# A two-block transformer kernel: the opening, both mixing branches and their gates written as one stage

## The reference, cut to what matters

```
mod = silu(c) @ w_ada + b_ada;  sh1, sc1, g1, sh2, sc2, g2 = split(mod, 6)
h = rmsnorm(x, norm_mix) * (1 + sc1) + sh1
rq, rk, rv, rg, dq, dk, dv, gate_r, gate_d = split(h @ w_in)
ro = retention(rope(rq), rope(rk), rv)              # 4 heads, 128 / 256 wide
ret_out = (head_rms(ro) * silu(rg)) @ w_ret_o
do = softmax(q1 k1) v - lam * softmax(q2 k2) v      # causal, 4 heads
diff_out = (head_rms(do) * diff_norm * 0.8) @ w_diff_o
merged = sigmoid(gate_r) * ret_out + sigmoid(gate_d) * diff_out
x = x + g1 * (merged @ w_out)
```

## Time and profile before

| | us |
|---|---|
| median of 3 runs | 3007.53 |
| profiled execution | 3010.33 |
| its span | 3008.6 |
| TensorE busy in the span | 2784.9 |
| VectorE busy | 2032.0 |
| first product matmul of the first block starts at | 74.58 |
| last product matmul of the changed part ends at | 767.9 |

### The profile page before, as it was taken

One profiled execution on the slowest core, in us unless ns is written; L12 is line 12 of the kernel. 1 busy time (PEld: TensorE's weight loads), 2 busy tenths in 40 slices (PEclk: granted clock), 3 DMA queues, 4 the chain that ended last, 5 costly groups with the idle time before them and its releaser, 6 DMA issues. The chain is left out here.

```text
span 3008.6 us, 36105 instructions
## 1 busy us (share of the span) xinstructions
PE 2784.9 (93%) x14003; PEld 2438.9 (81%) x14003; DVE 2032.0 (68%) x2760; ACT 1376.3 (46%) x1853; POOL 955.8 (32%) x499
## 2 busy tenths in 40 slices
PE   5979898679799999998898899989999999999999
PEld 4747786357578888886386689989999999999999
DVE  4436572522378988985166369998888768888884
ACT  2213212322267787775134233448788733333332
POOL 0414443024112222231122135633333344444430
PEclk7989999789699999999988999999999999999999
DMA  5315522012289999997431224559999999999993
GB/s 208 109 49 202 197 84 84 0 42 70 101 308 365 380 390 371 357 359 300 189 121 36 70 71 126 178 169 327 352 350 341 348 375 359 377 374 374 369 366 109
DMA packets 171261, 703.98 MB, mean 234 GB/s; under 512 B 24624, under 2 KB 51920, under 8 KB 134736
## 3 DMA queue, kind: packets, MB, share of 16 engines
q1 hardware_dynamic: 87696, 460.01, 41.8%
q0 software_dynamic: 47232, 142.66, 12.8%
q10 hardware_dynamic: 36160, 98.97, 8.8%
HBM read 658.03 MB, written 72.88 MB: 243 GB/s over the span
## 5 line engine op out<-in xcount | busy, mean ns | idle before, releaser
L188 PE MATMUL psum<-h_high,pe_high 128*128 128x384 f32 (+1 forms) x1664 | 570.1, 343 | 11.5 <-DVE h_low L2404 9.2
L190 PE MATMUL psum<-h_high,pe_low 128*128 128x384 f32 (+1 forms) x1664 | 564.1, 339 | 0.0
L189 PE MATMUL psum<-h_low,pe_high 128*128 128x384 f32 (+1 forms) x1664 | 564.1, 339 | 0.0
L2140 ACT ACTIVATE pe_high<-ring 128x1024 fp32r<-128x1024 f32 x272 | 287.1, 1056 | 326.4 <-PE psum L190 326.2
L2267 DVE TENSOR_TENSOR pe_low<-ring,pe_high 128x1024 fp32r<-128x1024 f32 x216 | 264.5, 1225 | 199.1 <-ACT pe_high L2140 196.4
L167 POOL TENSOR_TENSOR slab_low<-half_slab,slab_high 128x1024 fp32r<-128x1024 f32 x88 | 219.3, 2496 | 502.2 <-ACT slab_high L158 472.2
L188 PEld LDWEIGHTS psum<-h_high,pe_high 128*128 128x128 f32 x1664 | 313.4, 188 | 17.3 <-issue 10.0
L1335 DVE TENSOR_TENSOR slab_low_moe<-half_slab_moe,slab_high_moe 128x2048 fp32r<-128x2048 f32 x126 | 285.7, 2288 | 52.1 <-ACT slab_high_moe L1284 52.1
L190 PEld LDWEIGHTS psum<-h_high,pe_low 128*128 128x128 f32 x1664 | 313.0, 188 | 5.2
L189 PEld LDWEIGHTS psum<-h_low,pe_high 128*128 128x128 f32 x1664 | 313.4, 188 | 4.6
L2025 POOL DMA_INDIRECT pe_rows<-in_v_rows,pe_place x128 | 203.9, 1593 | 257.8 <-DVE pe_sums L2374 222.5
(11 more groups left out here) (452 smaller groups left out, 5993.3 us busy)
## 6 DMA issues: line engine op xcount, KB each, us to landing
half_slab_moe<-in_weights SPq DMA_DIRECT2D x128, 1024.0 KB, 7.3
ring<-in_weights SPq DMA_DIRECT2D x162, 512.0 KB, 5.5
hT<-in_weights SPq DMA_DIRECT2D x64, 1024.0 KB, 7.3
ring<-in_v_rows SPq DMA_DIRECT2D x128, 512.0 KB, 7.2
half_slab<-in_weights SPq DMA_DIRECT2D x44, 1024.0 KB, 5.1
gates_rows<-pe_table ACTq DMA_DIRECT2D x12, 2048.0 KB, 10.5
pe_gt<-gates_rows ACTq DMA_DIRECT2D x16, 1536.0 KB, 23.3
gelu_rows<-pe_gl ACTq DMA_DIRECT2D x30, 768.0 KB, 5.9
```

What stands on the lines that cost most here:

```text
L188: pe.matmul(out, w[0], x[0], start=start, stop=False)
L189: pe.matmul(out, w[0], x[1], start=False, stop=False)
L190: return pe.matmul(out, w[1], x[0], start=False, stop=stop)
L2140: act.activation(high[:, g % RING, :], raw[:, g % RING, :], ACT.Copy).then_inc(highs, 1)
```

## The change

All seven blocks become one block, `stage_mixer`, with one semaphore for each hand-over and no barrier within.

- Opening. The shift part is no longer made on TensorE: w_shift and L352 go, and VectorE makes all 16 dot products (`dots(0)` to `dots(7)`, 1 MB of w_ada each, six buffers). The small loads change their order (the rope positions last, the table's inputs earlier), and the widening of the table's input goes from GpSimd to ScalarE. The squares go ahead of every other small ScalarE step but the silu. The rope angles and sines come after the split of h. The scaling and the remainder are interleaved by chunks (`scale_chunk(k + 1)`, `low_chunk(k)`), and the first product tile waits for each chunk by itself (`split`). GpSimd makes the first quarter of slab 0 early and the next three once six chunks of h are split.
- Retention. `scores(0)` go between the k slab and the v slabs, `scores(1)` behind the v slabs; in the loop, output(i), then scores(i + 2), then the sum of squares. The sum of the last head goes behind the first tile of the silu gate. The decay table loads behind slab 1.
- Gates and output of retention use banks 4 to 7, the next projection banks 0 to 3. The sigmoid goes straight into `merged` (a copy of 512 columns on VectorE for each of 8 tiles goes). The 32 dot products take 0.5 MB each from a ring of four, spread 1, 2, 1 a tile over 24 tiles instead of 2 over 16. c is not loaded and activated again.
- Attention. Units run in the order t = 0, 3, 1, 2. Scores(0) and (1) go ahead of the v slabs. In the loop, scores(u + 2) go before swap(u) (the transposes), needing only the exponents of unit u. Five of the eight gate tiles are computed between the units, in steps of one chunk (three matmuls), 3, 3 and 2 steps in turn. Their results are copied out by ScalarE, the sigmoids are taken in one row later. The split of a head's result into high and low comes within the loop for heads 0 to 2.
- The last two stages (output, joint output) keep their order of products.

```diff
+            r_scores_of(0)
+            tokens(S_RV, r_turned, 4)
+            tokens(S_RV + 1, r_valued, 0)
+            r_scores_of(1)
+            for i in range(HEADS):
+                r_output(i)
+                if i + 2 < HEADS:
+                    r_scores_of(i + 2)
+                if i + 1 < HEADS:
+                    r_total_of(i)
...
+            pe.wait_ge(merged_by, 8)
+            pe.wait_ge(d_turned, 10)
+            d_scores_of(0)
+            d_scores_of(1)
+            tokens(S_DV, d_turned, 12)
+            tokens(S_DV + 1, d_valued, 0)
+            steps = iter([(n, k) for n in range(FILLED) for k in range(DC)])
+            for u, (i, t) in enumerate(units):
+                if u + 2 < len(units):
+                    d_scores_of(u + 2)
+                if t == ORDER[0] and i >= 1:
+                    d_output(i - 1)
+                if t == ORDER[1] and i >= 1:
+                    d_total_of(i - 1)
+                for _ in range(STEPS[u]):
+                    n, k = next(steps)
+                    gate_steps(n, (k,))
+                swap(u)
+            d_output(HEADS - 1)
+            gate_steps(FILLED, range(0, 3))
+            d_total_of(HEADS - 1)
+            gate_steps(FILLED, range(3, DC))
+            for n in range(FILLED + 1, 8):
+                gate_steps(n, range(DC))
...
+            for t in range(6):
+                dots(t)
+            dve.wait_ge(root, 1)
+            chain(dve.reciprocal(rstd, rstd))
+            dots(6)
+            dots(7)
...
+            scale_chunk(0)
+            for k in range(DC):
+                if k + 1 < DC:
+                    scale_chunk(k + 1)
+                low_chunk(k)
...
+            for u, (i, t) in enumerate(units):
+                if u + 1 < len(units):
+                    softmax_max(u + 1)
+                mix(u)
+                if t == ORDER[2] and i >= 1:
+                    d_norm(i - 1)
+                if t == ORDER[3] and i >= 1:
+                    do_lows(i - 1)
```

More of the change, by code:

```diff
@@ L206, in pe_tokens @@
[L206 to L219, removed]
@@ new lines, in _ @@
+            pe.wait_ge(const_in, 16)
+            for k in range(DC):
+                pe.wait_ge(squares_sem, k + 1)
+                mm = pe.matmul(m.bank[4][:, :], m.ones, work[:, k, :], start=(k == 0), stop=(k == DC - 1))
+            mm.then_inc(total, 1)
+            pe.wait_ge(rel_widened, 1)
+            for i in range(SWA_HEADS):
+                if i >= 3:
+                    pe.wait_ge(dist_sb, i - 2)
+                pe.matmul(m.bank[5 + i % 3][:, 0:VEC], rel_wide[:, i, :], buckets, start=True, stop=True).then_inc(dist_mm, 1)
@@ L546, in _, with dots @@
             chain = lambda instruction: m.chain(dve, instruction)
+            def dots(t):
+                dve.wait_ge(ada_in[t % 6], 16 * (t // 6 + 1))
+                first = ada_columns(t)[0]
+                for i in range(2):
+                    chain(dve.tensor_tensor_reduce(
+                        out=junk, in0=ada[t % 6][:, i * D:(i + 1) * D], in1=c_act, scale=1.0,
+                        scalar=0.0, op0=ALU.mult, op1=ALU.add, accum_out=m.raw[:, first + i:first + i + 1]))
+                dve.sem_inc(dotted, 1)
@@ new lines, in r_norm, with mod_dots @@
+            def r_norm(i):
+                dve.wait_ge(r_root, i + 1)
+                chain(dve.reciprocal(r_std, r_std))
+                for c in range(2):
+                    last = dve.tensor_tensor(roT[:, 2 * i + c, :], r_bank[i % 2][c][:, :], r_std, ALU.mult)
+                last.then_inc(r_normed, 1)
+            def mod_dots(first, count):
+                for n in range(first, first + count):
+                    dve.wait_ge(ring_in[n % 4], 16 * (n // 4 + 1))
+                    chain(dve.tensor_tensor_reduce(
+                        out=junk, in0=ada_ring[n % 4], in1=c_act, scale=1.0, scalar=0.0, op0=ALU.mult, op1=ALU.add,
+                        accum_out=m.raw[:, 16 + n:17 + n]))
+                    dve.sem_inc(ada_used, 1)
+                return first + count
@@ L762, in total @@
-            def total(h):
-                pe.wait_ge(s.squares, 2 * (h + 1))
-                if h >= 1:
-                    pe.wait_ge(s.root, h)
-                for c in range(2):
-                    mm = pe.matmul(ss_bank[:, :], m.ones, squares[:, c, :], start=(c == 0), stop=(c == 1))
-                mm.then_inc(s.total, 1)
-            scores(0)
-            scores(1)
-            for u, (h, t) in enumerate(units):
-                if t == 0 and h >= 1:
-                    output(h - 1)
-                turn(u)
-                if u + 2 < len(units):
-                    scores(u + 2)
-                if t == 1 and h >= 1:
-                    total(h - 1)
@@ L869, in stage_route @@
+            for i in range(8):
+                m.wait_product(dve, S_OUT + i // 4, i % 4)
+                dve.scalar_tensor_tensor(out=m.xT[:, i, :], in0=m.bank[i % 4][:, :], scalar=m.mod[:, 16 + i:17 + i],
+                                         in1=m.xT[:, i, :], op0=ALU.mult, op1=ALU.add).then_inc(mix_done, 1)
 def stage_route(nc, m, xT, hT, scale, shift):
```

1131 lines of the change are left out of this document (521 added, 610 removed).

## The result

| | before | after |
|---|---|---|
| median, 4 runs each | 3007.82 (3006.81 to 3011.51) | 2896.52 (2893.23 to 2899.65) |
| ratio, 95% interval | 1 | 0.9628 (0.9611 to 0.9644) |
| profiled execution, its span | 3010.33, 3008.6 | 2899.65, 2897.6 |
| first product matmul starts | 74.6 | 43.9 |
| last joint output product ends | 767.9 | 654.4 |

The change takes 111.3 us away, where 119.8 were forecast. The profiled executions differ by 110.7 us, the changed part by 113.5. The untouched part behind it took 2240.7 us before and 2243.2 after; over the fourteen kernels profiled here it lay between 2236.4 and 2243.8, though its code is the same in all. So effects of a few us are read inside the changed part.

What follows compares the result with a forecast made beforehand. TensorE, busy 2784.9 of 3008.6 us, was taken as the bound, losing time to waits and low clock in opening, retention and attention. Savings 25.7 + 21.3 + 10.2 + 6.8 + 55.8 = 119.8 gave 2888 us, range 2874 to 2904 (8 in 10: 2862 to 2925).

Steps and rivals of the forecast that it cites:

- opening, first projection: Start to first projection's end, 167.0 us before: shift leaves TensorE, chunks start products earlier; 25.7 saved, bounds 15 to 30.
- retention: Retention, 59.3 us before: barriers out, scores moved ahead, 38.0 left with 3.5 of waits; 21.3 saved, bounds 14 to 24.
- gates, retention output: Gates and retention's output, 140.7 us before: VectorE's load, barrier and split wait go, six dense slabs 130.5; 10.2 saved.
- attention, gates, its output: Attention through its output, 215.0 us before: 24 us a head, loop 89.5, total 159.2; 55.8 saved, bounds 45 to 67.
- L352 goes: Opening: TensorE's 27.5 us of shift at half clock vanish; VectorE's eight more dots and a read cost some 10.4 us.
- by chunks: Opening: one scaling and one remainder per chunk of h; first chunk reaches TensorE at 41.9, the eighth put at 56.
- The collision with GpSimd: Opening's split: GpSimd's three quarters after chunk six meet VectorE; 2.07 us for one meeting, 2.1 added.
- the serial piece: Attention, each head: sum of squares, root, 4.9 us VectorE block, maximum, mix; about 10 us, 3 to 3.5 added.
- R1: Attention runs at TensorE's own pace, 67 saved there for 55.8; 135 saved in all, 2873 us; chance 0.14.
- R2: Attention: the chain in a unit stays the bound, 40 to 16 saved there instead of 55.8; 2915 us; chance 0.18.
- R3: Opening gives nothing: VectorE's dots or collisions move h back to 74.5, 25.7 less saved; 2913 us; chance 0.04.
- R4: Slower: interleaved stretches and slabs behind hold TensorE's clock at 0.50, some 20 us more a slab; 3048; chance 0.04.

Runs made afterwards that it cites:

- before_no_shift: Kernel before with 8 of its 64 one-column shift products on TensorE (features 128 to 1023 left out): ratio 0.9926 to the kernel before.
- first_tile_whole: Changed kernel where the first product tile waits for all eight chunks of h: ratio 0.9652 to the kernel before (changed kernel 0.9628).
- joint_by_chunks: Changed kernel; joint output's first tile waits chunk by chunk, ScalarE rounds the merged tile before the weights' next quarter: ratio 0.9607 to the kernel before (changed 0.9628).
- root_early: Changed kernel with ScalarE's root of a head's sum moved ahead of the copy of that unit's transposes: ratio 0.9601 to the kernel before (changed 0.9628).
- before_scores_first: Kernel before with attention's scores(u + 2) moved ahead of the output and transposes of unit u: ratio 0.9904 to the kernel before.

## Why the prediction was right, point by point

| stretch | saved, forecast | saved, measured |
|---|---|---|
| opening, first projection | 25.7 | 28.0 |
| retention | 21.3 | 23.8 |
| gates, retention output | 10.2 | 8.6 |
| second projection | 6.8 | 6.4 |
| attention, gates, its output | 55.8 | 50.8 |
| joint output | 0 | -4.1 |
| sum | 119.8 | 113.5 |

2888 us was forecast and 2896.5 came, inside the forecast's own 2874 to 2904. Part of that closeness is luck: two stretches saved 4.8 us more than priced and four saved 11.1 less.

The measured column compares the ends of the same slabs in both traces; scores(0) of retention (2.2 us) and scores(0), (1) of attention (2.2) are counted with their own stretch, as in the forecast.

*Opening.* First product forecast near 42, came at 43.9: the 1.9 us are the meeting of the `mod` addition with GpSimd's early first quarter (2.07 us for 0.17), a collision that the sum didn't have at this place. The first tile forecast to end at 57, ended at 55.5, because the chunks of the split follow each other in 1.33 us, not in the 1.5 to 1.75 priced; slab 0 forecast to end at 74.3, ended at 71.9. The second v slab's end, forecast near 144, came at 141.3, most of it slab 0's. Here too is some luck: in four of the kernels with the same opening TensorE's granted clock fell again behind the split (0.57 to 0.77 from 54 to 58 us, 1.00 in the changed kernel), and slab 0 ended at 73.4 to 73.8. The step "L352 goes" is shown by before_no_shift (21.2 us in the first product's start), "by chunks" by first_tile_whole (6.7 at slab 0's end). The collision with GpSimd was there, 2.0 us at the split as priced.

*Retention.* 3.5 us for waits were forecast; TensorE stood 1.03 before output(0) and 1.17 before a sum, 2.2 in all. No experiment took this stretch apart. The clock of 1.00 for 0.87 and the two barriers (6.3 and 4.4 us) are read from the traces; how the 23.8 us divide between barriers and order is not shown.

*Gates.* No gap over 1 us, as said. Of the missing 1.6 us 1.3 lie in the two slabs of retention's output, which took 22.4 us each where a slab takes 21.76: their matmuls are 0.233 us apart, not 0.227. The cause isn't shown.

*Attention.* After the first head (17.4 us, priced at 17.5) heads of 24 us were forecast; 24.5 and 26.5 came, and 91.9 us for the loop, with the wait of 8.7 in it, where 89.5 were priced. That is 2.4 of the 5.0 us that this stretch missed. The last output (7.2 us, priced at 4.5) is 2.7 and attention's two output slabs (44.9 us, priced at 43.5) are 1.4; smaller pieces took 1.5 less than priced. The prediction's own signs were partly missed: the clock in the heads was 0.93, not over 0.95, and TensorE's largest wait there was still for the mix, 9.9 us in two waits, which it had named as the sign of being wrong in attention. (Two numbers in the prediction are off by a little: 1.3 meetings at 2.07 us are 2.7, not 2.8; four dots behind 33.4 end at 38.3, not 38.6. Neither decides anything.) The step that was mis-sized is "the serial piece", which I took as a root and one block of 4.9 us a head with 3 to 3.5 us showing. It is longer: the root stands behind a copy of transposes that TensorE hasn't made yet and behind a table load, so the norms waited 13.2 us in all. Moving the root ahead of the copy gave 12.9 us. At the loop's end, where no gate step is left (the last entry of the list is 0), the piece stood bare: 8.7 us, and the output behind it ran at a clock of 0.62.

*Joint output.* "Same products, same wait before them. 0." was wrong by 4.1. I compared TensorE's order and not ScalarE's: the change had turned rounding and weight splitting around there. joint_by_chunks gave 7.4 back, the rest of the old gap with it.

*The rivals.* R1 (TensorE's own pace, 135 saved) did not come true in the changed kernel, but root_early comes close to it: clock 1.00 and 43.8 us for two heads against its 41.4. R2 (the chain in a unit stays the bound) falls as a mechanism with before_scores_first, but not wholly as a size: the two heads' mean of 25.5 lies halfway between the 24 forecast and R2's 26.7, for another reason, the late root. R3 falls with the first product at 43.9. R4 falls: the clock's mean rose from 0.953 to 0.967. What the barriers carried is shown for one of six; the others weren't put back singly.

## What to carry to other kernels

Where one engine's stretch is full of waits of 3 us each on another that is itself half idle, look for the work item that is issued one step too late in the in-order queue and could have gone first. Moving one call gave 31 us in the kernel before and 11 in the changed one; twenty-seven us of filler gave 9 there. The two worked in the same holes, so the second of them to be added gives less than it would alone. Filler belongs where the longest wait is. Here that was the loop's end, beside the serial piece, and not every step evenly: 5.4 us of work put there gave 7.0. When stages are merged, compare the order on every engine, not only on the one that bounds: the joint output, whose products are the same, took 4 us more after a rounding step had changed places with a weight split.

## What the runs showed of the hardware that was not expected

- A VectorE instruction with a single SBUF input and one output was held up beside GpSimd as well: a tensor_scalar of 384 columns took 1.95 us for 0.42, a cast 2.61 for 0.43. I had priced meetings only for instructions with two SBUF inputs.
- The same untouched 2240 us of the program varied by 7.4 us between profiled executions of different kernels, more than the 3.4, 5.5, 6.9 and 7.0 us by which four of the edits tried here moved the part.
- After gaps of 4.4 and 5.3 us TensorE ran its next matmuls 0.43 us apart, at a granted clock of 0.50 (1.2 GHz), and the slab behind took 24.8 and 24.1 us instead of 21.9; after the gap of 3.05 us at the same place in the kernel before the clock stayed at 1.00. Such a stop costs more than its length.
- Ten kernels here have the same opening, and in those looked at TensorE waited 1.8 us for the last chunk of the split. In six kernels the granted clock was 1.00 from 54 to 58 us, just behind it, and slab 0 ended at 71.8 to 72.2; in four it was 0.57 to 0.77 and slab 0 ended at 73.4 to 73.8.
